# Two transformer blocks on one core: taking out the TensorE products whose result nobody reads

## The reference, cut to what matters

```
mix = token_mixing(x, ...)            # differential, compressed/selected/window attention, conv branch
x = layer_norm(ALPHA * x + mix, ln1_g[l], ln1_b[l])
ffn = conv_ffn(x, ...)
x = layer_norm(ALPHA * x + ffn, ln2_g[l], ln2_b[l])
```

```
t = rglru_mixer(hn, ...)  or  rwkv7_mixer(hn, ...)
x = x + rms_norm_2(t, g[1])
c = mem_cross_attention(rms_norm_2(x, g[2]), mem_n, c_w_q[i], c_w_kv[i], c_w_o[i])
x = x + rms_norm_2(c, g[3])
m = sqrelu_mlp(rms_norm_2(x, g[4]), m_w_up[i], m_w_down[i])
x = x + rms_norm_2(m, g[5])
```

## Time and profile before

| what | value |
|---|---|
| median of three runs | 3470.68 us |
| the profiled execution, its own time | 3467.44 us |
| its span, first to last instruction | 3465.6 us |
| mean granted TensorE clock over the span | 0.999 |
| TensorE busy (matmul) | 3429.6 us, 99% of the span |
| VectorE, ScalarE, GpSimd busy | 1654.5, 1411.1, 1388.4 us |
| data from and to memory | 317.43 MB, 92 GB/s |

### The profile page before, as it was taken

How to read it: one execution, slowest core, us unless ns; L and a number is a source line. 1 busy time by engine, 2 the same in 40 slices (tenths; PEclk the granted TensorE clock), 3 DMA queues, 4 the chain that set the end, 5 groups by cost and what they waited for, 6 DMA issues and landing times.

```text
span 3465.6 us, 52494 instructions
## 1 busy us (share of the span) xinstructions
PE 3429.6 (99%) x19196; PEld 2691.9 (78%) x19196; DVE 1654.5 (48%) x2657; ACT 1411.1 (41%) x2843; POOL 1388.4 (40%) x1112
## 2 busy tenths in 40 slices
PE   9999999999999999999999999999999999999999
PEld 7877787888788777888887777788874677868887
DVE  2566666442335765764424643422257874433032
ACT  3245534332333454343325643533317254444232
POOL 4632244444455222544454153444410222425444
PEclk9999999999999999999999999999999999999999
DMA  4421122222324111222232331222233321213222
GB/s 145 127 86 56 55 80 98 97 96 99 101 95 137 56 56 61 98 91 96 95 106 97 104 104 58 100 97 97 96 129 99 91 64 57 97 55 110 97 97 86
DMA packets 105274, 317.43 MB, mean 92 GB/s; under 512 B 27008, under 2 KB 31232, under 8 KB 104192
## 3 DMA queue, kind: packets, MB, share of 16 engines
q1 hardware_dynamic: 93168, 301.00, 26.0%
q10 hardware_dynamic: 11920, 13.85, 1.5%
HBM read 304.32 MB, written 7.34 MB: 90 GB/s over the span
## 4 chain that ended last, share of the span: by engine, by line
PE 92%; DVE 3%; DVEq 1%; DMA 1%; ACT 1%; issue 1%; SPq 0%; POOL 0%; ACTq 0%; POOLq 0%
PE ps L587 24%; PE ps L589 24%; PE ps L588 24%; PE ps L1343 2%; PE ps L1058 2%; PE ps L776 2%; PE ps L796 1%; PE ps L628 1%; PE ps L623 1%; PE ps L821 1%; PE ps L624 1%; DMA ring<-in_weights 1%; PE ps L1128 1%; PE ps L1162 1%; PE ps L1289 1%; PE ps L1227 1%
## 5 line engine op out<-in xcount | busy, mean ns | idle before, releaser
L3314 POOL TENSOR_TENSOR ring_r<-ring,rounded_r 128x512 fp32r<-128x512 f32 x505 | 670.0, 1327 | 1800.9 <-ACT rounded_r L1622 1791.9
L587 PE MATMUL ps<-source_hi,rounded_r 128*128 128x512 f32 x2360 | 933.2, 395 | 3.5 <-DVE Y_lo L3249 1.9
L588 PE MATMUL ps<-source_hi,ring_r 128*128 128x512 f32 x2360 | 919.5, 390 | 0.0
L1622 ACT ACTIVATE rounded_r<-ring 128x512 fp32r<-128x512 f32 x512 | 323.4, 632 | 1305.0 <-PE ps L589 1141.6
L3316 POOL TENSOR_TENSOR ring_r<-ring,rounded_r 128x512 fp32r<-128x512 f32 x505 | 701.5, 1389 | 0.0
L589 PE MATMUL ps<-X_lo,rounded_r 128*128 128x512 f32 x1456 | 568.1, 390 | 0.0
L587 PEld LDWEIGHTS ps<-source_hi,rounded_r 128*128 128x128 f32 x2360 | 443.2, 188 | 116.7 <-issue 21.3
L588 PEld LDWEIGHTS ps<-source_hi,ring_r 128*128 128x128 f32 x2360 | 443.6, 188 | 90.5 <-issue 1.9
L589 PEld LDWEIGHTS ps<-X_lo,rounded_r 128*128 128x128 f32 x1456 | 273.4, 188 | 58.1
L1623 ACT ACTIVATE rounded_r<-ring 128x512 fp32r<-128x512 f32 x512 | 316.5, 618 | 0.0
L589 PE MATMUL ps<-N_lo,rounded_r 128*128 128x512 f32 x760 | 296.1, 390 | 0.0
(11 more groups left out here) (534 smaller groups left out, 5511.5 us busy)
## 6 DMA issues: line engine op xcount, KB each, us to landing
ring<-in_weights SPq DMA_DIRECT2D x556, 512.0 KB, 3.3
X<-in_x SPq DMA_DIRECT2D x4, 512.0 KB, 6.7
PAIR<-Z ACTq DMA_DIRECT2D x32, 64.0 KB
residual<-X ACTq DMA_DIRECT2D x1, 2048.0 KB, 9.4
X<-residual SPq DMA_DIRECT2D x1, 2048.0 KB, 9.6
ring<-in_weights SPq DMA_DIRECT2D x16, 128.0 KB, 2.6
SWAP<-Z ACTq DMA_DIRECT2D x4, 256.0 KB, 5.8
MEM<-in_mem ACTq DMA_DIRECT2D x1, 1024.0 KB, 4.8
```

The source lines that it names most:

```text
L587: mm(o, lh, rh, start=start, stop=False)
L588: mm(o, ll, rh, start=False, stop=False)
L1622: av(RH[:, j, FRONT], ring[:, j, FRONT], ACT.Copy).then_inc(w_hi_half, 1)
L3314: nc.gpsimd.tensor_tensor(RL[:, j, FRONT], ring[:, j, FRONT], RH[:, j, FRONT].bitcast(F32), ALU.subtract).then_inc(w_lo_half, 1)
```

## The change

All calls of `warm` are removed. Nothing is added, and nothing else is moved; `warm` itself stays defined and is called by nobody. The lines that go:

```diff
                 sums_of(l, 0, KT - 1)
-                warm(7, 1)
                 spread(l, 0)
-                warm(7, 2)
...
                 sums_of(l, 1, KT - 1)
-                warm(7, 1)
                 spread(l, 1)
-                warm(7, 2)
...
                 for c in range(1, RING):
                     values(c)
-                warm(0, 2)
                 gemm(B + RING, C_MQ, AH, NL, scaled, C_LRU_IN + l * KT, SRC[f"q{l}"], 0, 3 + 6 * l, skewed=True,
...
                 pe.wait_ge(mv, l * 4 + 4)
-                warm(4, 2)
                 pe.wait_ge(m_pt, l * 2 * ST + 2 * ST)
...
                 rms_out(4 + 6 * l)
-                warm(1, 1)
                 rms_spread(4 + 6 * l)
-                warm(3, 3)
...
                 end_sums(1)
-                warm(3, 1)
                 end_spread(1)
...
             pe.wait_ge(lru_gate, 16)
-            warm(3, 3)
             gemm(B_LRU_OUT, C_LRU_OUT, AH, ZL2[:, 16:24, :], t_ready, 0, SRC["lru_out"], skewed=True)
...
             pe.wait_ge(rw["yc"], RU - 1)
-            warm(0, 2)
 
             def last_turned():
                 gate(RU - 1)
                 turn_output(RU - 1)
-                warm(6, 2)
```

## The result

The changed kernel takes 3481.35 us (median of seven runs, 3475.68 to 3486.53) against 3470.7 (seven runs, 3469.92 to 3471.63) for the kernel before, run beside it. The ratio is 1.0028, with a 95% interval from 1.0019 to 1.0037: slower by 10.7 us, where 8.4 was forecast. The profiled execution took 3481.05 us, with a span of 3479.3; that is 13.6 over the profiled one of before, which lay 3.24 under its own median, while this one lies at its median.

What follows compares the result with a forecast made beforehand. TensorE, busy for 99% of the span, was taken as the bound. From the profiled 3467.4 us, -1.4 off the path and +9.8 for clock falls gave 3475.8; with the median 3.24 higher, 3479.1 us (+0.24%), range 3468.5 to 3489.

Steps and rivals of the forecast that it cites:

- The sum that comes off the path: Removed products' gain: -1.1 us ahead of four layer-norm spreads, -0.3 at the LRU output; -1.4 in all, ends 0 and -7.
- Gain 0 at the query product: Tails' query product, 2 places: what is won at the front is waited away for VectorE; at most 2.6 us for both.
- Number of falls: Seven falls of the granted clock: two at RWKV output, four in the tails, one at the fourth layer norm; ends none, eleven.
- between the two: Other layer norms and LRU output: 1.8 us idle or dense products close by, between emptiest places and stretches holding full clock.
- The first rival (the clock holds): Clock holds everywhere or falls at two places or fewer: not slower, 3469.3 us, up to 3472; chance 0.35.
- Price of a fall: Loss per fall of the granted clock at emptied places: 1.4 us, ends 0.5 and 2.0.
- the first part: Place-by-place reading of removed products: only those on the path gain; elsewhere TensorE waits for another engine, gain 0.
- The 4.0 us in the sum: Length of the low clock under dense work, read at the kernel's start; loses half, 2.0 us, if all falls on products.
- the 1.2 us put in: Part of a fall passed without loss, about half of an idle time of 1.8 to 2.9 us: (4.0 - 1.2) / 2.
- The signs named ahead: 19124 matmul records, PEclk under 1.00 in or just behind named places, products there 0.43 us apart, mean clock 0.995.
- the count is right by accident: What the prediction said would hold if the clock fell at other places than the ones it named.
- the falls' +9.8: Total loss from seven falls at 1.4 us each, in the tails, RWKV output and fourth layer norm; ends none and 22.

Runs made afterwards that it cites:

- keep_ln: Changed kernel with the two products behind each layer norm's spread put back (4 x 2); 3478.4 us, ratio 1.0020.
- keep_rwo: Changed kernel with only the 4 products at the RWKV output put back; 3475.57 us, ratio 1.0016.
- no_mlp: Kernel before without the products around the MLP's spread in the two tails (2 x 4), all others kept; 3471.08 us, ratio 1.0004.
- no_rwo: Kernel before without the 4 products at the RWKV output, all others kept; 3473.77 us, ratio 1.0009.
- narrow: Kernel before with all 36 products kept, each with one column and not 512; 3477.82 us, ratio 1.0025.
- covers_lru: Kernel before without the products ahead of layer-norm spreads, at the query product and ahead of the last spread; LRU output's three stay; 3468.99 us, ratio 0.9998.
- covers: Kernel before without the products ahead of layer-norm spreads, at the LRU output, at the query product and ahead of the last spread; 3470.92 us, ratio 1.0001.
- keep_tails: Changed kernel with the products at the tails' attention output and around the MLP's spread put back (2 x 6); 3475.3 us, ratio 1.0017.
- before_xparts: Kernel before, all products kept, with the reload of X cut into four DMAs one RWKV unit apart; 3469.62 us, ratio 0.9997.
- best: Kernel before without the 9 products ahead of spreads and query products, 27 kept, and the reload of X cut in four; 3467.65 us, ratio 0.9991.
- covers_xparts: Kernel before without products ahead of layer-norm spreads and last spread, at LRU output and query product; reload of X cut in four; 3468.18 us, ratio 0.9996.
- after_xparts: Changed kernel with the 2048 KB reload of X cut into four DMAs one RWKV unit apart; 3478.48 us, ratio 1.0023.

## Why the prediction was right

**The sum that comes off the path.** Forecast -1.1 at the spreads and -0.3 at the LRU output; measured -1.0 and -0.1. The spreads behave as worked out, down to the wait of 0.33 and the 1.16 us of the eight records; all four gave 0.25 to 0.27. At the LRU output TensorE started early and stood for 2.22 us ahead of slot 2, until 0.1 us after GpSimd's part, as forecast. The 31.0 us of removed work brought 1.2.

**Gain 0 at the query product.** Here the ends were 0 and a gain; it was a loss of 0.4 and 0.3 us. TensorE did run 1.7 us ahead at the front and gave it all back, mostly in waits for VectorE's lower parts (0.38, 0.62 and 0.30 us in the first tail, name the row), as forecast, and a little more. In the first tail the little more is a weight chunk that came later: ahead of these rows ScalarE waits 2.09 us for it, and 1.69 in the kernel before, and VectorE waits for ScalarE. Why it came later stays open.

**Number of falls.** Seven forecast, eight found. Both at the RWKV output, both at the MLP, one of two at the attention's output, the fourth layer norm: six of the seven named. The first tail's attention output held in this profile and fell in `keep_ln`; the third layer norm fell, which I had put between the two. With falls at the LRU output too in `keep_rwo`, a place is better given a chance than a yes or no. The first rival (the clock holds) is out: seven runs, the fastest at 3475.68, and no profile of a kernel with emptied places at the RWKV output was without falls. The ground given for it, that no idle time is over 2.9 us, did not hold: at the emptied places falls stand behind idle times of 1.7 to 2.8 us.

**Price of a fall.** 1.4 us forecast. Where full-width products follow in rows it was 1.4 to 1.8 (third and fourth norm, RWKV output, attention's output). At the MLP it was 0.25: there the term of the sum was mis-sized, by 2 x 1.15 = 2.3 us. The products stand 0.43 us apart there as well (2201.23 - 2200.80), but TensorE comes to a wait of 0.89 us for ScalarE 6 us later and would have stood there anyway. I had charged all the time that a fall takes from TensorE to the path, after having shown in the first part that this is not so for a removed product. `no_mlp` bears it out for a fall of 3.4 us (0.1 us in its profile) and shows the limit: the one of 6.8 us cost 1.2, since the waits there take back 1.3 us and no more.

Half of the recorded 3.41 us is 1.7 us a fall, an estimate from that length and the distances of 0.85 and 0.43 us shown below. The profiles agree for dense stretches (1.4 to 1.8) and not at the MLP (0.25), since it is an estimate of TensorE's time and not of the kernel's.

The 4.0 us in the sum are what one start of the kernel took. In the trace of before the record of the clock begins at 5.50 us, with 1.00 (stretches ahead of it read 1.00 for want of an entry), and there the plain products of 512 columns go over from 0.85 us apart to 0.43. In the changed kernel's fall at 3049.91, where PEclk is 0.50, such products stand 0.85 us apart too (3052.22 - 3051.36). The first four rows are of the kernel before, the last two of the changed one:

```profile
4.19 1.06 PE L833 MATMUL ps<-RS 128*128 128x512 f32 x1
5.05 0.82 PE L833 MATMUL ps<-RS 128*128 128x512 f32 x1
6.14 0.59 PE L833 MATMUL ps<-RS 128*128 128x512 f32 x1
6.57 0.59 PE L833 MATMUL ps<-RS 128*128 128x512 f32 x1
3051.36 1.06 PE L1156 MATMUL ps<-Z 128*128 128x512 f32 x1
3052.22 1.06 PE L1156 MATMUL ps<-Z 128*128 128x512 f32 x1
```

From the first product, at 1.47, to 5.50 are 4.0 us. But that is one start of many and no bound: in the 14 profiles the record begins at 4.71 to 7.60 us, with the products ahead of it 0.85 us apart from the second on, so the low clock lasted 3.2 to 6.1 us under the same products. The falls took 3.41 us, but 6.83 in four places and 10.24 in one. With 3.41 in place of 4.0, the sum's form gives 1.1 us a fall and not 1.4; what dense stretches lost was 1.4 to 1.8, so less of a fall passed without loss than the 1.2 us put in.

**What was missing.** The recurrence: a wait of 3.7 us and a fall behind it, +5.0 us in all. No product was taken out there, and I had read its rows only for the clock. The signs named ahead held elsewhere (19124 records, mean clock 0.995, falls in or just behind the named places), but "the count is right by accident" is true in part: without the recurrence the falls' +9.8 would have stood against 8.4 measured, and the kernel at about 5 us less in the profile. From profile to profile the forecast was +8.4 and the result +13.6. That the medians are only 10.7 apart comes from a profiled execution before that lay 3.24 us below its median, while the one after lay at its own. The total was met by luck in part: a term too large, one missing, and this. One slip besides: 1 - 7 x 4.0 x 0.5 / 3475 is 0.996; it is 0.995, as forecast and found, when taken off the 0.999.

**What the wait is** was narrowed down, not proved. All 14 profiles, for the recurrence from 2780 to 2892 us (time of before):

| kernel | products missing ahead | longest wait without a semaphore | clock low | against before |
|---|---|---|---|---|
| before | 0 | 1.0 us | 0 us | 0 us |
| `no_rwo` | 0 | 0.9 | 0 | +1.9 |
| `narrow` | 0, but one column each | 0.7 | 3.4 | +3.0 |
| `no_mlp` | 4 | 0.9 | 0 | +1.8 |
| `covers_lru` | 6 | 2.0 | 3.4 | +4.2 |
| `covers` | 9 | 2.0 | 0 | +1.5 |
| `keep_ln` | 15 | 4.3 | 10.2 | +8.0 |
| `keep_tails` | 17 | 1.2 | 0 | +1.0 |
| `keep_rwo` | 23 | 3.3 | 6.8 | +4.6 |
| changed | 23 | 3.7 | 3.4 | +5.0 |
| `before_xparts` | 0, cut transfer | 0.8 | 0 | +2.1 |
| `best` | 6, cut transfer | 1.1 | 0 | +1.8 |
| `covers_xparts` | 9, cut transfer | 0.7 | 0 | +0.9 |
| `after_xparts` | 23, cut transfer | 0.8 | 0 | -0.1 |

The long waits stand where many products are missing, but not in order: `keep_tails` lacks more than `covers` and waits less. The times of the packets come nearer to a cause: in nine profiles TensorE goes on 1.2 to 1.4 us after the end of a 16 KB packet of instructions. In the changed kernel 7.5 us lie between the end of the packet before and the start of this one (2793.58 to 2801.04), 5.0 in the kernel before. That fits instructions which are fetched in blocks (16 KB a packet), and a block's end that moves against the transfer's start when instructions are taken out ahead of it; that the transfer holds the packet up is argued from this and not shown. With the cut transfer no wait near 2800 is over 0.6 us, and waits of 0.7 to 1.1 us stand 17 to 55 us later, which end 1.3 to 1.6 us after a packet of instructions. The cut changes the size of the transfer, its start and SP's waits together; which of the three removes the wait is not shown.

## What to carry to other kernels

Useless products in TensorE's idle times can be worth their place: here 27 of them cost nothing and, with the reload cut in four, keep the clock in ten runs of 11; the 9 that stand ahead of a ready product gain about 1 us when taken out, which the profiles show at the spreads (0.25 to 0.27 each) and no median here can. Judge each by two questions: does TensorE go on at once when it is gone, and what stands behind it when the clock is low, full-width products in rows (1.4 to 1.8 us) or TensorE's next wait (0.25, as long as that wait is not used up)? And set both lists of products side by side from start to end, since one of the largest terms of this change was in a stretch that it does not touch. And set more than one profile of the kernel before beside it: between profiles, stretches without any edit moved by up to 2 us.

## What the runs showed that I had not expected

- Idle times of 1.7 to 2.8 us with a few products around them were enough for the clock to fall, also with dense work on both sides (2.13 us at the LRU output in `keep_rwo`), and not in each execution: the same place holds in one profile and falls in another.
- Products of one column did not keep the clock: with 72 records of 0.25 us in place of 0.59 it fell nine times, and eight times with none at all.
- A 2 MB transfer seems to hold up TensorE's own instruction stream (waits of 0.9 to 4.3 us without a semaphore, 0.7 to 1.1 and later with the transfer cut in four). Its signs in the profile are an idle time with no releaser, and a packet of the instruction queue that ends 1.2 to 1.4 us ahead of the wait's end.
- Runs of the changed kernel spread over 10.9 us, those of the kernel before over 1.7 beside it and over 8.7 in the largest group (33 runs). Each run has its own set of falls: the changed kernel's mean clocks are 0.993 to 0.995, lowest in its slowest run (3486.53). By the 3.4 us of a fall and the 6 us at the end that is an estimate of 8 to 12 falls, where the profiled run, at 0.995, has eight.
